# Sums stored tile by tile, and expert matrices asked for place by place, in a hybrid decoder layer with 64 experts

## The reference, cut to what matters

```python
    for l in range(DEPTH):
        mix = hybrid_mixer(h, ...)
        h = layer_norm(DN_ALPHA * h + mix, ln1_g[l], ln1_b[l])
        ffn = moe(h, router_w[l], router_b[l], exp_w_gu[l], exp_w_down[l], sh_w_gu[l], sh_w_down[l])
        ple = jax.nn.sigmoid(h @ ple_w_g[l] + ple_b_g[l]) * (p[l].astype(h.dtype) @ ple_w_e[l])
        h = layer_norm(DN_ALPHA * h + ffn + ple, ln2_g[l], ln2_b[l])
```

## Time and profile before

| | us |
|---|---|
| median of 3 runs (lowest to highest) | 2556.87 (2556.73 to 2560.52) |
| profiled execution, its own time | 2556.02 |
| its span | 2553.9 |
| PE busy in the span | 2440.9 (96%) |
| DVE, ACT, POOL busy | 892.5, 437.3, 805.1 |

### The profile page before, as it was taken

How to read it: one execution, slowest core, us unless ns; L and a number is a source line. 1 busy time by engine, 2 the same in 40 slices (tenths; PEclk the granted TensorE clock), 3 DMA queues, 4 the chain that set the end, 5 groups by cost and what they waited for, 6 DMA issues and landing times. The chain is left out here.

```text
span 2553.9 us, 26598 instructions
## 1 busy us (share of the span) xinstructions
PE 2440.9 (96%) x10446; PEld 1482.6 (58%) x10446; DVE 892.5 (35%) x1522; ACT 437.3 (17%) x689; POOL 805.1 (32%) x764
## 2 busy tenths in 40 slices
PE   6999999999999999999999999979999999999992
PEld 3444554345799544444444544457777777787761
DVE  5001653675533523323323262222222223323324
ACT  1001122335454100010000110001111111111112
POOL 3000111101343100000001125425666666767654
PEclk9999999999999999999999999989999999999996
DMA  6201003100000211011050411069999999999995
GB/s 258 83 33 48 19 33 104 41 17 9 1 1 26 91 50 50 25 50 50 25 205 26 156 63 50 26 257 350 343 349 347 345 346 345 342 348 342 348 350 178
DMA packets 168027, 391.36 MB, mean 153 GB/s; under 512 B 19770, under 2 KB 40298, under 8 KB 167136
## 3 DMA queue, kind: packets, MB, share of 16 engines
q1 hardware_dynamic: 135312, 300.64, 32.2%
q0 software_dynamic: 31584, 82.00, 12.4%
q10 hardware_dynamic: 1008, 7.02, 0.7%
HBM read 322.50 MB, written 67.11 MB: 153 GB/s over the span
## 5 line engine op out<-in xcount | busy, mean ns | idle before, releaser
L1860 PEld LDWEIGHTS banks<-arena 128*128 128x128 f32 x4096 | 523.8, 193 | 75.2 <-DMA arena<-in_exp_w_gu 39.0
L1860 PE MATMUL banks<-arena 128*128 128x128 f32 (+7 forms) x4096 | 533.8, 292 | 30.4 <-DMA arena<-in_exp_w_gu 28.1
L2295 POOL DMA_INDIRECT arena<-hp_scratch,arena x306 | 294.9, 964 | 242.4 <-issue 80.8
L1380 PE MATMUL banks<-arena 128*128 128x512 f32 x672 | 293.2, 597 | 1.3 <-PEq L736 1.3
L328 PE MATMUL banks<-arena 128*128 128x512 f32 x640 | 280.9, 596 | 4.6 <-DVE arena L1093 4.3
L1868 PE MATMUL banks<-arena 128*128 128x512 f32 (+1 forms) x528 | 237.4, 592 | 1.3 <-DVE arena L2254 0.9
L1380 PEld LDWEIGHTS banks<-arena 128*128 128x128 f32 x672 | 128.5, 191 | 163.7 <-issue 163.7
L328 PEld LDWEIGHTS banks<-arena 128*128 128x128 f32 x640 | 120.3, 190 | 159.1 <-issue 149.4
L280 POOL TENSOR_SCALAR arena<-arena 128x1 f32<-128x1 f32 x16 | 15.5, 971 | 606.1 <-DVE arena L271 606.1
L2310 POOL DMA_INDIRECT acc_scratch<-arena x99 | 153.7, 1552 | 66.3 <-DMA acc_scratch<-arena 41.3
L321 PE MATMUL banks<-arena 128*128 128x512 f32 x384 | 167.7, 595 | 0.6 <-PE banks L321 0.6
(11 more groups left out here) (372 smaller groups left out, 2536.9 us busy)
## 6 DMA issues: line engine op xcount, KB each, us to landing
arena<-in_exp_w_gu SPq DMA_DIRECT2D x64, 2048.0 KB, 24.6
arena<-in_exp_w_down SPq DMA_DIRECT2D x64, 1024.0 KB, 18.9
arena<-in_w_in SPq DMA_DIRECT2D x10, 2048.0 KB, 9.0
arena<-in_w_in SPq DMA_DIRECT2D x12, 1024.0 KB, 6.1
arena<-in_w_branch SPq DMA_DIRECT2D x12, 512.0 KB, 7.1
hp_scratch<-arena SPq DMA_DIRECT2D x10, 512.0 KB, 2.8
arena<-hp_scratch,arena POOLq DMA_INDIRECT x306
arena<-in_x SPq DMA_DIRECT2D x4, 1024.0 KB, 14.7
```

The lines of the kernel that those rows point to most:

```text
L1380: last = nc.tensor.matmul(PS[:, g % 4, :], lhs[:, k, :], rhs[:, k, :], start=(k == 0), stop=(k == 3))
L1860: last = nc.tensor.matmul(PS[:, bank + part, f * n:(f + 1) * n], weights[:, k, part * FF + f * P:part * FF + (f + 1) * P], x[:, k, 0:n], s ...
L2295: nc.gpsimd.indirect_dma_start(out=rows[0:n, :], out_offset=None, in_=table, in_offset=bass.IndirectOffsetOnAxis(ap=at, axis=0)).then_inc( ...
```

## The change

The store of `acc` is cut in eight DMAs, one for each token tile, each issued when the last embedding job of that tile is added; they count on four semaphores, one for two tiles. `weights_in` is cut in two functions, `gate_up_in` and `down_in`. Gate and up of place 1 are asked for right behind the slot tables, those of place 2 ahead of the last tile's store. The down matrix of place r (1 to 4) waits only for the two tiles whose memory it takes. GpSimd's first addition to `acc_d` waits for all four semaphores. Both functions read the expert's number for themselves, so there are two register loads for each place.

```diff
+        f_st = [sem(f"f_st{i}") for i in range(NT // 2)]
...
-                def weights_in(r):
+                def gate_up_in(r):
                     e = table(sp, rank_e, r, NE - 1)
                     if r == 0:
                         sp.wait_ge(f_dn, 2 * NT)
...
                     else:
                         sp.wait_ge(x_u, r - RING + 1)
                     sp.dma_start(gu[r % RING], gu_v[bass.ds(e, 1)].rearrange("a p k n -> p (a k) n")).then_inc(x_wg[r % RING], 16)
+
+                def down_in(r):
+                    e = table(sp, rank_e, r, NE - 1)
                     if 0 < r < RING:
-                        sp.wait_ge(f_st, 16)
+                        sp.wait_ge(f_st[r - 1], 32)
                     elif r:
                         sp.wait_ge(x_dn, chunks(r - RING + 1))
                     sp.dma_start(dn[r % RING], dn_v[bass.ds(e, 1)].rearrange("a p f n -> p (a f) n")).then_inc(x_wd[r % RING], 16)
 
+                def sums_out(t):
+                    sp.wait_ge(f_pr, NT + t + 1)
+                    sp.dma_start(acc_d[t * P:(t + 1) * P, :], acc[:, t, :]).then_inc(f_st[t // 2], 16)
+
                 sp.wait_ge(e_tab, 1)
-                weights_in(0)
+                gate_up_in(0)
+                down_in(0)
...
-                sp.wait_ge(f_pr, 2 * NT)
-                sp.dma_start(acc_d[0:SEQ, :].rearrange("(t p) d -> p t d", p=P), acc).then_inc(f_st, 16)
-                for r in range(1, NS):
-                    weights_in(r)
+                gate_up_in(1)
+                for t in range(NT):
+                    if t == NT - 1:
+                        gate_up_in(2)
+                    sums_out(t)
+                    if t >= 3 and t % 2:
+                        down_in(t // 2)
+                for r in range(3, NS):
+                    gate_up_in(r)
+                    if r >= 4:
+                        down_in(r)
...
                     else:
-                        pool.wait_ge(f_st, 16)
+                        for done in f_st:
+                            pool.wait_ge(done, 32)
```

More of the change, by code:

```diff
@@ L1578, in build @@
         f_w, f_p, f_bg, f_wg, f_we = (sem("f_" + n) for n in ("w", "p", "bg", "wg", "we"))
-        f_gu, f_sl, f_up, f_hid, f_dn, f_acc, f_tp, f_pT, f_pl, f_lg, f_sg, f_pr, f_chain, f_st, f_sl2, f_slq, f_stp, f_int = (
-            sem("f_" + n) for n in ("gu", "sl", "up", "hid", "dn", "acc", "tp", "pT", "pl", "lg", "sg", "pr", "chain", "st",
+        f_gu, f_sl, f_up, f_hid, f_dn, f_acc, f_tp, f_pT, f_pl, f_lg, f_sg, f_pr, f_chain, f_sl2, f_slq, f_stp, f_int = (
+            sem("f_" + n) for n in ("gu", "sl", "up", "hid", "dn", "acc", "tp", "pT", "pl", "lg", "sg", "pr", "chain",
                                     "slots_in", "slots_quad", "slots_t", "slots_int"))
+        f_st = [sem(f"f_st{i}") for i in range(NT // 2)]
         x_wg, x_wd = ([sem(f"x_w{n}{i}") for i in range(RING)] for n in "gd")
```

## The result

| | before | changed |
|---|---|---|
| median (lowest to highest), us | 2556.80 (2556.64 to 2560.52), 4 runs | 2537.71 (2536.05 to 2539.19), 4 runs |
| profiled execution, its span | 2556.02, 2553.9 | 2537.53, 2535.4 |
| ratio to before | | 0.9925 (95% interval 0.9912 to 0.9937) |

What follows compares the result with a forecast made beforehand. The DMA stream was taken to set the experts' end, with PE only a little faster. 20.3 us for moved bytes plus 1.3 for an earlier start gave 21.6 us less, 2534.9 us forecast, range 2528 to 2542.

Steps and rivals of the forecast that it cites:

- What bounds the kernel: In the experts, the DMA stream sets the end and PE is only a little faster; both must move.
- PE, 19.7 us: At the experts' start, PE begins place 2 at 1701.4 instead of 1721.13, without the 17.4 us wait and lower clock.
- The absolute 1701.4: Predicted start of place 2 on PE: 1686.3 + 11.7 for place 1 + 3.4 for down of place 0.
- The start of the stream, 1.3 us: Near 1680, gate and up of place 2 wait only for the last embedding matmul, so the stream starts 1.3 us earlier.
- 7.86 MB at 2.58 us per MB, 20.3 us: Stores and matrices moved ahead of 1680 leave the busy DMA stream; priced from queue shares, they are worth 20.3 us.
- Both together: In the experts, PE moves 19.7 us and the stream 21.6; 1.9 us of PE's late losses make up the difference.
- the queue running dry: In the experts, the stream's lead over PE grows only 1.9 us; 4.9 of 6.8 us of queued work remain.
- The additions at nothing: Seven more stores and waits on SP, second register loads and POOL's extra waits are hidden and cost nothing.
- Less of it: Rival: something of places 1 to 4 comes late, about 2540, up to 2548; chance 0.12.
- More of it: Rival: the stream is not the bound in the experts, PE alone counts, 32 us gained, 2524; chance 0.08.
- The time stays: Rival: matrices land early but the stream's share is made up elsewhere, so the end does not change; chance 0.04.
- slower: Rival: second register load on SP's path sets the rate in the experts, 44 us lost, 21.6 won, 2578; chance 0.04.

Runs made afterwards that it cites:

- e7: Changed kernel with PE doing gate and up of place 40 twice (64 more matmuls): 2538.72 us, ratio to before 0.9923.
- e5: Changed kernel with seven more down-matrix loads (7.34 MB) into unread memory, behind every third place from 10 to 28: 2556.76 us, ratio to before 0.9988.
- e8: Kernel before with only gate and up of place 1 asked for early, behind the slot tables, all sums in one store: 2553.24 us, ratio 0.9986.
- e11: Changed kernel with gate and up of place 1 asked for late, at about 1679 us: 2541.77 us, ratio to before 0.994.
- e9: Changed kernel with the down matrix of place 3 asked for ahead of gate and up of place 2: 2533.54 us, ratio to before 0.9908.
- e10: Changed kernel with one register load instead of two for each place from place 3 on: 2536.70 us, ratio to before 0.9918.
- e6: Changed kernel with seven more down-matrix loads (7.34 MB) between the matrices of place 0 and the slot tables: 2560.38 us, ratio to before 1.0003.
- e1: Kernel before with only gate and up of place 1 asked for early, on a chip where before took 2674 us: ratio 0.9946.
- e2: Changed kernel with gate and up of place 1 asked for late, on a chip where before took 2674 us: ratio to before 0.9978.
- e4: Changed kernel with place 3's down matrix ahead of place 2's gate and up, on a chip where before took 2674 us: ratio 0.9973.
- e12: Changed kernel with seven more loads (7.34 MB), one behind each of the first seven stores: 2662.18 us where before took 2671.66, ratio 0.9963.
- e3: Changed kernel with one register load for each place from place 3 on, on a chip where before took 2674 us: ratio 0.991.

## Why the prediction was right, and which term was too large

**What bounds the kernel.** Shown from both sides, on chips where before takes 2557 to 2559 us: 8.3 us more of PE cost nothing that can be measured (e7), 7.34 MB more of DMA cost 17 us (e5), and an early start of PE with only 2.10 MB less in the stream gave back 9 of its 13 us (e8).

**PE, 19.7 us.** Exact. Place 2 starts 22.3 to 22.5 us after place 0 instead of 42.2. The absolute 1701.4 came out as 1701.9, because the embedding ended 0.7 us later in that run. Gathers and matrices of places 2 and 3 were in time; PE has no wait until 2285.

**The start of the stream, 1.3 us.** 1679.44 against 1680.09, with that 0.7 us in it: right.

**7.86 MB at 2.58 us per MB, 20.3 us.** This is the term that was mis-sized. The length fell by 19.0; less 1.3 for the start that leaves 17.7 us, or 2.25 us per MB. The experiments agree: e5 17.2 us for 7.34 MB (2.35), e11 4.9 us for 2.10 MB (2.3), e8 4.2 for 2.10 MB (2.0), e9 1.8 for 1.05 MB (1.7); the last two rest on small differences of single profiles. So the price of one more MB is about 2.3 us, some 10% under the average that I took from the shares. What lies behind it is seen only in part. The queues over the whole stretch, before (1680 to 2480), changed (1680 to 2461), and the weight queue of e5 (1680 to 2479):

```profile
q1 hardware_dynamic: 82781, 200.40, 67.6%
q0 software_dynamic: 27952, 77.19, 36.3%
```

```profile
q1 hardware_dynamic: 80221, 192.36, 66.7%
q0 software_dynamic: 27952, 77.19, 37.3%
```

```profile
q1 hardware_dynamic: 82152, 199.75, 67.5%
```

The time of the weight packets is 0.676 x 800 / 200.40 = 2.699 us per MB before and 0.667 x 781 / 192.36 = 2.708 changed. Each MB that stayed became 0.3% dearer, 1.7 us in all, while the same gathers (77.19 MB) took a larger share of a shorter time; with the seven loads back (e5) it is 0.675 x 799 / 199.75 = 2.700 again. The shares are printed to 0.1%, so the 1.7 us can be off by 0.8 us. Scaled to 100% as in the prediction (the shares of all queues add to 104.2% and 104.4%), the two prices are 2.590 and 2.594, which is only 0.8 us. So this points the right way and may be a part of the missing 2.6 us; the rest stays open. That denser gathers are what makes the weight packets slower was not tested.

**Both together, and the queue running dry.** The stream gained 19.0 where PE gained 19.7, so PE's late waits grew by 0.5 instead of falling by 1.9, and the down matrices landed 1.1 us later instead of earlier. The DMA share stayed at 1.05. Nothing ran dry.

**The additions at nothing.** The second register loads cost no more than a measurement can tell (e10, by its length). No run takes the eight stores by themselves; the trace has their times from issue to landing:

```profile
DMA to landing us min/median/max: 2.6/3.2/11.5
```

The first took 10.2 us beside gate and up of place 1, the next six 2.6 to 4.4 us, with jobs 8.6 us apart, and only the last (11.5 us) stood in the busy stream. The fixed cost of about 2 us for each DMA that the prediction quotes from the Trainium skill ("DMA: Bandwidth & Descriptors", section "Anatomy of one DMA") was not on the path of these stores. That section is about DMAs that GpSimd issues, and these are SP's; no run here shows what a fixed part of theirs would cost on the path.

**The rivals.** "Less of it" by late rows did not happen. "More of it" did not: the 383 GB/s in 1704 to 1740 fell to 353 once gathers were there. "The time stays" and "slower" fell with the result, and the length of e10 puts the mechanism of the last at under 1 us.

## What to carry to other kernels

When DMA engines and a compute engine are both full, read what each has behind the last idle stretch: what is gained is the smaller of two amounts: what the DMA stream moves, and what the compute engine moves plus the waits for that stream that it still has to give (e8: 5.4 us by the prediction's price against 13.4 and more, and 4.2 came out). Bytes moved ahead into an idle stretch are worth their time even where nothing waits for them individually, but only if that stretch holds no chain of DMA latencies; the same seven loads cost some 21 us beside 64 dependent scatters. The price of moved bytes is better taken from a run with bytes added than from the average share: here it was 10% less.

An order that follows the same thought one step further (e9, the down matrix of place 3 also ahead) took 2533.54 us and was 1.8 us shorter in the experts. It is the one that I would keep, though so small a gain is not beyond doubt.

## What had not been expected of the hardware

- Seven loads of 1 MB beside a chain of small scatters made POOL wait 54.1 us instead of 30.2 for their landings, and moved its end by 22 us, with the DMA engines not full there (their share in e6 was 0.84 in 1542 to 1560, 0.63 in 1560 to 1580 and 0.42 in 1580 to 1600).
- On two chips the same program took 2665 to 2696 us instead of 2557. In e1, on one of them, the experts moved 327 GB/s in 1740 to 2090 where 345 had been usual (307 to 313 in e2 to e4 and e12), and PE had 57.3 us in 97 gaps for which the profile shows no releaser ("issue"), with no wait put down to a matrix:

```profile
1740.00:2090.00 350.00, 336.64 (x1875) 258.68 (x1874) 84.08 (x141) 36.46 (x63) 214.54 (x201) 0.97 1.01 327
```

```profile
PE banks L1865 <- issue: 57.3, 97, 7.1
```

What slowed them stays open. On the first of these chips the kernels also come in another order: against before, e1 gained 14 us by the medians, e3 24, e4 8 and e2 6, where the other chip gave 4, 21, 24 and 16. So the account above, in which the stream sets the end, is shown for chips on which before takes 2557 to 2559 us, and not for these.
